# Three transposes of a DeltaNet step moved from TensorE to VectorE and a trip through memory

## The reference

```
qkv = silu(causal_conv(concat(dq, dk, dv)));  dq, dk = l2norm(dq), l2norm(dk)
L   = strict_lower((k*beta) @ k.T * decay);   solve (I + L) u = v*beta, (I + L) w = k*beta*exp(gc)
per chunk, in order:
    v_new = u_n - w_n @ state
    o     = q_n @ state + attn_n @ v_new
    state = state * exp(gl) + k_n.T @ v_new
o_d = o_d * rsqrt(mean(o_d**2) + EPS) * dn_g;  o_d = o_d * silu(dz)
```

## Time and profile before

| what | value |
|---|---|
| median of 3 runs | 2643.95 us |
| profiled execution, its time | 2642.51 us |
| profiled execution, span in the trace | 2640.7 us |
| TensorE busy | 2621.0 us, 99% of the span |
| VectorE busy | 1734.6 us, 66% |
| ScalarE busy | 739.8 us, 28% |
| GpSimd busy | 800.0 us, 30% |
| mean granted TensorE clock | 0.999 of full speed |
| DMA packets, data | 293417, 217.80 MB |

### The profile page before, as it was taken

The page is one execution under the profiler, slowest core; times in us unless marked ns, Lnnn a source line. Parts: engine busy times, 40 slices in busy tenths (PEclk is TensorE's granted clock), DMA queues, the critical chain, the costliest instruction groups (busy, mean ns, idle before and its releaser), DMA issues.

```text
span 2640.7 us, 40598 instructions
## 1 busy us (share of the span) xinstructions
PE 2621.0 (99%) x14874; PEld 2240.1 (85%) x14874; DVE 1734.6 (66%) x3908; ACT 739.8 (28%) x1888; POOL 800.0 (30%) x451
## 2 busy tenths in 40 slices
PE   8999999999999999999999999999999999999998
PEld 6888888888888899888878888888888998888887
DVE  7878777877755555434578778777877555653333
ACT  6333333333312212200143333333332211230001
POOL 3123333333312212434422333323322122132453
PEclk9999999999999999999999999999999999999999
DMA  5321222122211112423523222222222111133344
GB/s 175 99 86 56 83 68 87 53 86 65 85 51 43 41 35 74 131 93 117 165 85 98 73 78 65 73 77 74 69 73 73 43 51 43 41 107 101 98 136 152
DMA packets 293417, 217.80 MB, mean 82 GB/s; under 512 B 31746, under 2 KB 246100, under 8 KB 292964
## 3 DMA queue, kind: packets, MB, share of 16 engines
q1 hardware_dynamic: 259620, 159.07, 20.5%
q10 hardware_dynamic: 33600, 56.15, 6.2%
HBM read 176.30 MB, written 38.86 MB: 81 GB/s over the span
## 4 chain that ended last, share of the span: by engine, by line
PE 94%; DVE 2%; DMA 1%; ACT 1%; issue 1%; SPq 0%; ACTq 0%; DVEq 0%; POOL 0%
PE dense_ps L866 24%; PE dense_ps L870 23%; PE dense_ps L868 23%; PE work L849 3%; PE dense_ps L890 2%; PE dense_ps L891 2%; PE dense_ps L892 2%; PE work L1145 1%; PE work L1182 1%; PE work L1104 1%; PE work L1202 1%; PE work L1121 1%; PE work L1171 1%; PE work L1195 1%; PE work L1156 1%
## 5 line engine op out<-in xcount | busy, mean ns | idle before, releaser
L866 PE MATMUL dense_ps<-act_hi,w_hi 128*128 128x512 f32 x2552 | 1048.2, 411 | 1.6 <-DVE w_lo L1801 0.8
L870 PE MATMUL dense_ps<-act_hi,w_lo 128*128 128x512 f32 x2552 | 998.2, 391 | 0.0
L868 PE MATMUL dense_ps<-act_lo,w_hi 128*128 128x512 f32 x2552 | 997.2, 391 | 0.0
L2577 POOL TENSOR_TENSOR w_lo<-w_raw,w_hi 128x1024 fp32r<-128x1024 f32 x162 | 400.7, 2473 | 1022.5 <-ACT w_hi L1429 579.3
L870 PEld LDWEIGHTS dense_ps<-act_hi,w_lo 128*128 128x128 f32 x2552 | 479.0, 188 | 105.9
L866 PEld LDWEIGHTS dense_ps<-act_hi,w_hi 128*128 128x128 f32 x2552 | 481.1, 189 | 86.4 <-POOL act_lo L2598 2.3
L868 PEld LDWEIGHTS dense_ps<-act_lo,w_hi 128*128 128x128 f32 x2552 | 481.5, 189 | 78.5 <-issue 0.5
L1977 DVE SCALAR_TENSOR_TENSOR arena<-arena,cols 128x512 f32<-128x512 f32 x288 | 245.4, 852 | 6.1
L1429 ACT ACTIVATE w_hi<-w_raw 128x1024 fp32r<-128x1024 f32 x94 | 99.1, 1054 | 329.3 <-PE dense_ps L870 310.4
L1419 ACT ACTIVATE arena<-dense_ps 128x512 f32<-128x512 f32 x96 | 57.3, 597 | 258.5 <-PE dense_ps L870 258.5
L849 PE MATMUL work<-mk,arena 128*128 128x128 f32 x768 | 113.4, 278 | 6.8 <-DMA arena<-in_x 6.8
(11 more groups left out here) (262 smaller groups left out, 4150.9 us busy)
## 6 DMA issues: line engine op xcount, KB each, us to landing
w_raw<-in_w_in SPq DMA_DIRECT2D x138, 512.0 KB, 3.6
arena<-l_scratch SPq DMA_DIRECT2D x64, 256.0 KB
arena<-gate_scratch ACTq DMA_DIRECT2D x64, 256.0 KB, 2.7
gate_scratch<-arena ACTq DMA_DIRECT2D x36, 256.0 KB, 2.0
w_raw<-in_w_out SPq DMA_DIRECT2D x18, 512.0 KB, 3.5
o_scratch<-arena ACTq DMA_DIRECT2D x32, 256.0 KB, 2.2
w_raw<-in_w_up_dn SPq DMA_DIRECT2D x16, 512.0 KB, 3.4
arena<-o_scratch ACTq DMA_DIRECT2D x32, 256.0 KB, 3.6
```

The source lines that it names most:

```text
L866: eng.matmul(dense_ps[:, to, :], w_hi[:, slot, k, :], hi[:, k, seg], start=(k == 0), stop=False)
L868: eng.matmul(dense_ps[:, to, :], w_hi[:, slot, k, :], lo[:, k, seg], start=False, stop=False)
L870: mm = eng.matmul(dense_ps[:, to, :], w_lo[:, slot, k, :], hi[:, k, seg], start=False, stop=(k == KT - 1))
L2577: eng.tensor_tensor(w_lo[:, slot, :, :], w_from[second][:, :, :], w_hi[:, slot, :, :].bitcast(F32), ALU.subtract)\
```

## The change

Three kinds of turns leave TensorE: `ob` in the 28 even and odd steps of heads 0 to 6 (both layers), `kt` in the same steps except the even step of head 0 in each layer, and `vt` in the 14 even steps. In their place VectorE transposes 32x32 blocks inside a 128x512 tile (`turn_v`, `turn_k`, `turn_o`) into a buffer `turned`; ScalarE's queue stores them (`put`, 4 DMAs in slot 15) to a scratch tensor in memory so that the 32x32 blocks come to lie in their turned places, in runs of 32 numbers (128 bytes); and one DMA (`get`, slot 19) loads them back as rows of 128 numbers into `tokens`. VectorE reads `tokens` in slot 22 of the same step: for the values (`vt`, even steps), the gated output (`ob`) and the keys of the step after the next (`next_keys`, which takes the place of `kt`). The store of the gated output moves to slot 2 of the next step (`late_store`). Three semaphores are joined into one to make room.

```
-        at(18, "store")
+            at(18, "store")
+        if kind in ("even", "odd", "even_last"):
+            at(2, "late_store")
...
-        at(vt, "vt")
+        at(22 if kind == "even" else vt, "vt")
...
+    if kind in ("even", "odd"):
+        at(14, "turn_k")
+    if kind == "even":
+        at(12, "turn_v")
...
-        begin(15, 1, ("ob",))
+        begin(15, 1, ("turn_o",))
+        at(15, "put")
+        at(19, "get")
+        at(22, "ob")
+        at(22, "next_keys")
...
+        turned = arena[:, swap_at:swap_at + BACK * HALF].rearrange("p (m s) -> p m s", s=32)
+        tokens = arena[:, swap_at + BACK * HALF:swap_at + 2 * BACK * HALF].rearrange("p (x c t) -> p x c t", x=BACK, c=CPH)
...
+        back_dram = nc.dram_tensor("back_scratch", [CPH * CPH * BACK, 32, P], F32)
...
+                        elif what == "put":
+                            u = back(l, h, b)
+                            ms = slice(0, (BACK if kind == "even" else BACK - 1) * CPH * CPH)
+                            eng.wait_ge(on_ok.sem, on_ok.after(t, BACK + 1))
+                            eng.wait_ge(back_in.sem, back_in.after(u, 0))
+                            for i in range(CPH):
+                                rows = slice(32 * i, 32 * i + 32)
+                                eng.dma_start(back_dram[ms, :, rows].rearrange("m r s -> r m s"), turned[rows, ms, :])\
+                                   .then_inc(back_st.sem, 16)
+                        elif what == "get":
...
+                            eng.wait_ge(back_st.sem, back_st.after(u, 64))
...
+                            eng.dma_start(tokens[:, 0:(BACK if kind == "even" else BACK - 1)].rearrange("p x c t -> p (x c) t"),
+                                          back_dram[ms, :, :].rearrange("(m j) r d -> (j r) m d", j=CPH))\
+                               .then_inc(back_in.sem, 16)
...
+                        elif what == "turn_o":
+                            eng.wait_ge(on_ok.sem, on_ok.after(t, BACK))
+                            eng.transpose(turned_of(BACK_O), on.rearrange("p c t -> p (c t)")).then_inc(on_ok.sem, 1)
...
+                        elif what == "next_keys":
...
+                            eng.wait_ge(back_in.sem, back_in.after(back(l, h, b), 16))
+                            eng.wait_ge(st_ps.sem, st_ps.after(t, CPH))
+                            eng.tensor_tensor(kd[b], tokens[:, BACK_K], per_token(hs[:, 3, CPH * b:CPH * b + CPH]), ALU.mult)\
+                               .then_inc(kd_ok.sem, 1)
```

More of the change, by code:

```diff
@@ L47 @@
 HBUF = 4
+BACK = 3
+BACK_O, BACK_K, BACK_V = range(BACK)
+BACK_UNITS = 2 * (DH - 1)
 def in_order(*steps):
@@ L2205, in delta_unit @@
                                 eng.wait_ge(zeros_ok.sem, zeros_ok.after(l, 2))
-                            eng.wait_ge(kt_ps.sem, kt_ps.after(tn, 1))
+                            if kind == "odd" or kind == "even" and h:
+                                continue
+                            eng.wait_ge(kt_ps.sem, kt_ps.after(3 * l + ("first", "even", "even_last").index(kind), 1))
                             if t is not None:
```

89 lines of the change are left out of this document (74 added, 15 removed).

## The result

The changed kernel takes 2723.01 us (median of 4 runs, 2716.53 to 2725.01), the kernel before 2645.68 in the same runs: ratio 1.0288, 95% interval 1.0264 to 1.0311. The forecast was 2666 us and slower; the sign was right, the size (+22 forecast, +77 measured) was not. The time lies just inside the widest range that the prediction names (2622 to 2725), at the end where it put its third rival. The profiled execution has a span of 2714.4 us against 2640.7, and a mean granted clock of 0.986 against 0.999.

What follows compares the result with a forecast made beforehand. TensorE, busy 99%, bounds the kernel, with VectorE close behind at the even step's end. 14 pairs x (2.3 - 0.7) + 0.7 = 23 us on 2642.5 gives 2665, 2666 as median; forecast 2650 to 2700, widest range 2622 to 2725.

Steps and rivals of the forecast that it cites:

- third rival: Short stores of put are dear, 30.5 ns a packet: even-step stall 8.7 us, 2741 us; chance 0.20 for 2700 and up.
- What TensorE saves: Turns taken off TensorE save 1.14 us per even step and 0.70 per odd one, 25.1 us in all.
- VectorE's transposes: Each 128x512 transpose on VectorE takes 0.69 us, adding 2.1 us in an even step and 1.4 in an odd one.
- the landing of `put`: In the even step, put takes 8.0 us to land in memory, bounds 5.9 and 13.4 us.
- The even step's stall: At the even step's end TensorE waits 3.4 us for uu, making the step 2.3 us longer.
- ScalarE now issues 4 DMAs: In the even step, put's four issues take ScalarE 1.9 us at 0.48 each, leaving z_silu 0.3 us later than before.
- The odd step: Its trip is hidden in VectorE's idle 5.78 us, saving 0.70 us; block stores and reloads for the solve cost nothing.
- The clock: Under the third rival's long stall, TensorE idle for so long may be granted less clock, adding time; no size given.
- All is hidden: VectorE's added work finds room and the trip is short: 2619 us, partly hidden up to 2635; chance 0.20.

Runs made afterwards that it cites:

- e18: e12 with the last head's way back in its own step, and a silu, value scale and convolution step behind recurrence products in odd steps: 2633.8 us, ratio 0.9955.
- e1: Changed kernel with the four transfers of each put issued by SyncE, not ScalarE: 2707.2 us, ratio 1.0233.
- e14: Changed kernel with ScalarE's puts moved from slot 15 to slot 17, behind the gate's tanh and the weight split: 2701.8 us, ratio 1.0212.
- e3: Changed kernel with the trip cut to one 16 KB block each way, VectorE reading the turned tile, values not the reference's: 2673.2 us, ratio 1.0107.
- e10: e9 with the puts issued by ScalarE at slot 15, as in the changed kernel: 2696.2 us, ratio 1.0194.
- e9: e7 with the keys' step moved to slot 7, output to slot 10 and store to slot 12, except output and store in the last even step: 2655.5 us.
- e4: Changed kernel with the store of the normed output moved from slot 2 of the next step to slot 9: 2702.9 us, ratio 1.0218.
- e12: e9 with the way back issued at slot 3 of the next step instead of slot 21 of its own: 2654.5 us, ratio 1.0033.
- e8: Changed kernel with nine 128x128 matmuls before TensorE's wait for the scaled values in each odd step: 2710.0 us, ratio 1.0248.
- e7: e1 with values turned on TensorE, output and keys scaled at slot 2 of the next step, store at slot 9, way back at slot 21: 2668.5 us.

## Why the prediction was wrong, point by point

- **What TensorE saves (25.1 us): right as far as seen.** The balance above closes with it within some 3 us, and the pair of e18 gave three quarters of its share. No run measured it alone.
- **VectorE's transposes (0.69 us) and the landing of `put` (8.0 us): right,** 0.69 to 0.71 and 7.2.
- **The even step's stall (3.4 us): right in size by luck, wrong in cause.** 3.41 us at 424.61 and 2.9 on average. I had VectorE ready at 405.65 and waiting for a landing at 407.05, from which `uu` was to take 3.15 us (the five terms named for it add up to 3.0). The landing came about in time; VectorE was 2.4 us later than forecast, because of the next point. e1 and e14 show the landing close behind: with ScalarE free, `vt` waits for it.
- **The step that failed: "ScalarE now issues 4 DMAs: at the 3.80/8 = 0.48 us each ... that is 1.9 us".** I took the row of the block stores, 4 KB in 64 runs, for transfers of 1536 pieces. They took 2.9 to 4.6 us in even steps (mean 3.6) and 2.3 to 3.8 in odd ones (mean 2.8). At 0.43 us each the row would have been near for small transfers (e3: 1.73 us for four). `z_silu` started 5.0 us behind `turn_o`, where the forecast has 2.5. Worse, I followed the hold only to `z_silu`. It also holds the weight split, and so the block stores. Its price is 41 us in e10 against e9, and 16 us in e1 against the changed kernel, where the waits close behind it take up the rest.
- **The odd step ("nothing" for stores and reloads): failed.** "VectorE starts the solve some 4 us after they land" stands on no row. In the odd step of the kernel before the DMA engines are 0.28 busy from 410 to 411 us and idle from 411 to 412, and the solve starts at 413.15, some 2 us later. Three small delays use that up: the split behind the puts, the way back beside the block stores (the reload came 1.69 us behind the last store's issue, before 1.03; in e9 2.9), the output's store beside the reload (e4). VectorE's wait for the reload became 42.7 us (4.6 before), and as state updates stand in the same queue TensorE waited 21.3 us for them, in the even step too (387.04), where the prediction wanted no new wait. Moving the way back (e12) took the reload's wait from 34.3 to 10.3 us.
- **The clock: named only for the third rival, as what more a stall of 8.7 us might cost.** Stops of 2.2 and 3.4 us were followed by some 3 us at 1.2 GHz; the whole is 35 us, by the mean clock, and no term of the sum. e8 bought 0.010 of clock back by filling the stop.
- **Not in the prediction at all:** `ob` read PSUM before and SBUF after, so that it can be blocked by GpSimd; in the changed kernel it stood where GpSimd was idle (0.74 to 0.75 us each time), in e7 and in e9 not.
- **The rivals.** "All is hidden" asked for the data by 403.7; 12.6 us behind `turn_o` is 406.4 on that clock, and VectorE was later still. The third ended at the right size (2700 and up) for a reason that did not occur (dear short stores: 12.2 ns, not 30.5).

What stays open: how the loss divides among the causes. The balance of the single contributions is made with the clock, and they do not add up one by one, since each wait removed uncovers the next (71 us of waits in e1 against 64, at a time 16 us shorter).

## What to carry to other kernels

Price the issue of a DMA by its pieces (2.9 us for four of 1536 pieces, 1.7 for four of 32), and ask of each engine that issues it what stands behind in its queue, over the whole step and past it. Where TensorE is busy 99% of the time, a saving of 0.35 us is worth having only if VectorE's next product for it is 0.35 us early too: look for that margin first, and move whatever it doesn't need behind it. A two-operand VectorE step that moves from PSUM to SBUF operands belongs where GpSimd is idle, or where nothing that TensorE wants stands behind it (e18).

## What the runs showed of the hardware that was not expected

- Four DMA issues of 1536 pieces of 128 bytes took 2.93 to 2.95 us on ScalarE and 2.88 to 2.98 on SyncE, of 32 long runs each 2.07 to 2.09, of 32 pieces of 128 bytes 1.73 to 1.76: 0.30 us per transfer between 1536 pieces and 32. In the steps in which a 16 KB transfer of the queue `q8 instruction` moved at the same time they took some 1 us more, on either engine (up to 4.59 and 4.42).
- Steps of VectorE with all operands in SBUF took 1.53 or 1.78, 1.77 and 2.85 us beside GpSimd where they take 0.75, 0.69 and 0.69 alone; an in-place product of 128x4 took 1.48. A product of the same size that reads PSUM (`kt`, kernel before) took 0.69 beside GpSimd too.
- Pieces of 128 bytes stored to memory cost 12.2 ns of a DMA engine, and joined into wide ones they saved nothing where nobody waited for them (ratios 1.0037 and 1.0033).
